# Quads of 512-column passes for the token-major blocks of a transformer layer kernel

## The chip, the core and the metric

One Trainium2 chip; the program runs on one of its cores. The metric is the device time of one execution in microseconds (us). A core has TensorE (PE in the rows; its weight loads are PEld), VectorE (DVE), ScalarE (ACT), GpSimd (POOL) and SyncE (SP), which here only issues DMAs. Matmuls write to PSUM, eight banks of 128 partitions by 512 fp32; ACT and DVE read those banks. The engines run their own instruction lists and wait for each other through semaphores.

## The reference

One layer on x of 512 tokens by 1024, all in fp32. One wide projection `h @ w_in` feeds three things: a sparse attention in four groups of four heads (compressed, selected and window keys), a state-space mixer in four groups of eight heads, and two gates. Then two projections are gated and merged, projected out, and a gated feed-forward with a short convolution follows.

```python
h = rms_norm(x, norm1_w[layer])
(q, k_c, v_c, k_s, v_s, k_w, v_w, g_nsa, z, xbc, dt_raw,
 gate_a, gate_b) = split_columns(h @ w_in[layer], IN_SIZES)
y_a = nsa_mixer(q, k_c, v_c, k_s, v_s, k_w, v_w, g_nsa, ...)
y_b = ssd_mixer(z, xbc, dt_raw, ...)
merged = sigmoid(gate_a) * (y_a @ w_proj_a[layer]) + sigmoid(gate_b) * (y_b @ w_proj_b[layer])
x = x + merged @ w_out[layer]
x = x + conv_glu_ffn(rms_norm(x, norm2_w[layer]), ...)
```

The parts of it that the change touches are the columns q, k_s, v_s, k_w, v_w (the "heads" columns of a group: 128 + 128 for q and 64 each for the rest, 512 in all) and z (512 columns a group), which are wanted with tokens on the partitions.

## The kernel before, in words

**Weights.** Every weight matrix is cut into units of 512 KB, numbered in the order of use. SP loads unit u into one of two tiles `wraw` (it waits until unit u-2 is split: `load`). ACT rounds it to fp32r (`hi(u)`, L1029, into one of four slots of `w_high`), DVE forms the rest (`lo(u)`, L1553, `w_low`), and TensorE multiplies three times for each product: high by high, high by low, low by high. `hi(u)` waits until the block that last used the slot is done, and the loaded unit.

**Blocks.** Most units are 128 output columns by 1024 rows and make one block: 8 k-steps of three matmuls of 512 tokens (`ktile`, L611 to L613), weights stationary, into one of the two banks `g`. Blocks whose result is wanted token-major come in pairs (`half_pair`, L652 to L654): activations stationary, and the moving operand is the 128 columns of two units side by side, 256 columns a matmul. A pair is done in two halves of 48 matmuls, each half giving two of the four token tiles for 256 columns. There are 16 such pairs: 5 and 8 before the groups, four in each of groups 0 to 2 (two for the heads columns of the next group, two for z) and two in group 3 (z only; its other four blocks of that place are gate columns, of the ordinary kind).

**A group.** The main stretch runs over g = 0..3, 14 blocks each: OB, OC, eight blocks OQ+n (n = 0..7, the *turns*), and four OX blocks. Between the k-steps of a block TensorE does the small work of the attention, at places set by dictionaries `between`. A turn n belongs to unit n of the attention (head r = n // 2 and kind br = n % 2), and runs as follows:

- TensorE: scores of unit n+1 (L786), k-step 0, values of unit n-1 (L802) before k-step 1, the first two pieces of the transposed probabilities before k-step 3 (seven transposes, L604; they wait for `p_ready`), the third piece before k-step 6 (three transposes). The pieces use two banks `t` in turn, so the third waits until DVE has read the first (`t_rel`). In turn 0 the places are 2 and 5, in turn 7 they are 5 and 7.
- ACT: rounds each piece (`pT_hi`, L1333), does the exponentials of unit n+1 (`exps`, L1296), one first tap of the convolution (L1103), copies the block's bank out (`evac_mid`), then `hi(u+3)`.
- DVE: `scale(n)` (reciprocal L1837, four products L1843; gives `p_ready`), `ttr(n+1)` (score maxima, L1784), in turns 2, 4, 6 `out_fold` (L1874), `lo(u0+4+n)`, `p_low` on the first two pieces (L1855), `p_low` on the third, and from turn 2 on one convolution (`conv`, three instructions, L1603), then the next turn.

The order on each engine is the order written; no scheduler moves anything. In groups 1 to 3 turn 0 follows the normalized output of the group before (`y_back_out`: four copies on ACT, each with a DMA that stores it).

## Time and profile before

| | us |
|---|---|
| median of 3 runs | 1240.8 (1240.5 to 1240.89) |
| the profiled execution | 1241.02 |
| its span, first to last instruction | 1239.3 |
| PE busy in the span | 1225.5 (99%) |
| DVE busy | 841.5 (68%) |
| ACT busy | 633.1 (51%) |

TensorE's granted clock is 1.0 of full speed through the span. A matmul's duration in the records includes its way through the array and overlaps the next one's, so the cost of a matmul in a dense run is the distance between two starts. The busy share of DVE is a mean over the program: in the 80 us of a group's turns from 400 to 480 us it is busy for 69.75 us.

### The profile page before, as it was taken

The page shows a single profiled execution, that of the slowest core. Times are in us where ns is not written, and L with a number is a line of the kernel's source. Part 1 is how long each engine was busy: PE and PEld are TensorE (multiplying, and loading weights), DVE is VectorE, ACT ScalarE, POOL GpSimd, SP SyncE. Part 2 cuts the span into 40 slices and gives each one's busy share as a digit, 9 for nine tenths or more (in the row PEclk, how much of TensorE's full clock was granted, in tenths as well). Part 3 has the DMA queues.
Part 4 walks back from the last instruction along what each step waited for, and adds up shares of the span by engine and source line. Part 5 has one row for each costly group of instructions (what it writes and reads, how often), then busy time and mean ns, then how long its engine had stood idle before and what let it go on. Part 6 is the DMA issues. An engine that isn't in the chain of part 4 may idle for free.

```text
span 1239.3 us, 17708 instructions
## 1 busy us (share of the span) xinstructions
PE 1225.5 (99%) x6725; PEld 1053.5 (85%) x6725; DVE 841.5 (68%) x1579; ACT 633.1 (51%) x1169; POOL 88.8 (7%) x78
## 2 busy tenths in 40 slices
PE   7999999999999999999999999999999999999998
PEld 6998998899978998889978888888888888888887
DVE  4526888898889887999774643333788888884221
ACT  6615777678785868676765633323432322332210
POOL 1000001400042001400040000000000000000000
PEclk9999999999999999999999999999999999999999
DMA  8612321142213221132216633335133333334341
GB/s 241 162 35 68 86 61 46 49 108 63 61 44 80 75 70 51 51 103 61 61 34 212 230 96 92 90 104 175 56 102 102 87 100 102 92 97 136 102 130 40
DMA packets 185737, 116.34 MB, mean 94 GB/s; under 512 B 25933, under 2 KB 169909, under 8 KB 185653
## 3 DMA queue, kind: packets, MB, share of 16 engines
q1 hardware_dynamic: 182023, 108.86, 30.5%
q10 hardware_dynamic: 3630, 6.35, 1.4%
q8 instruction: 54, 0.88, 0.3%
q14 instruction: 30, 0.25, 0.1%
HBM read 106.80 MB, written 8.39 MB: 93 GB/s over the span
## 4 chain that ended last, share of the span: by engine, by line
PE 94%; DVE 4%; ACT 1%; issue 0%; ACTq 0%; DVEq 0%
PE g L611 17%; PE g L613 16%; PE g L612 16%; PE t L604 5%; PE g L652 4%; PE g L654 4%; PE g L653 4%; PE ob L802 3%; PE s L786 3%; PE s L960 2%; PE s L961 2%; PE s L962 2%; PE s L883 1%; PE t L708 1%; PE ob L920 1%; PE t L962 1%
## 5 line engine op out<-in xcount | busy, mean ns | idle before, releaser
L1029 ACT ACTIVATE w_high<-wraw 128x1024 fp32r<-128x1024 f32 x175 | 185.1, 1058 | 281.4 <-DMA wraw<-in_ffn_w_up 135.2
L1553 DVE TENSOR_TENSOR w_low<-wraw,w_high 128x1024 fp32r<-128x1024 f32 x174 | 216.7, 1248 | 125.2 <-ACT w_high L1029 122.7
L611 PE MATMUL g<-hT_hi,w_high 128*128 128x512 f32 x360 | 158.3, 440 | 1.2 <-DVE hT_lo L1559 1.2
L652 PE MATMUL g<-w_high,hT_hi 128*128 128x256 f32 x512 | 151.6, 296 | 0.2 <-DVE w_low L1553 0.2
L654 PE MATMUL g<-w_high,hT_lo 128*128 128x256 f32 x512 | 144.7, 283 | 0.0
L653 PE MATMUL g<-w_low,hT_hi 128*128 128x256 f32 x512 | 144.6, 282 | 0.0
L613 PE MATMUL g<-hT_hi,w_low 128*128 128x512 f32 x360 | 141.2, 392 | 0.0
L612 PE MATMUL g<-hT_lo,w_high 128*128 128x512 f32 x360 | 140.8, 391 | 0.0
L611 PE MATMUL g<-h2T_hi,w_high 128*128 128x512 f32 x352 | 137.4, 390 | 0.1
L613 PE MATMUL g<-h2T_hi,w_low 128*128 128x512 f32 x352 | 137.0, 389 | 0.0
L612 PE MATMUL g<-h2T_lo,w_high 128*128 128x512 f32 x352 | 137.0, 389 | 0.0
L653 PEld LDWEIGHTS g<-w_low,hT_hi 128*128 128x128 f32 x512 | 97.8, 191 | 0.5
L652 PEld LDWEIGHTS g<-w_high,hT_hi 128*128 128x128 f32 x512 | 97.6, 191 | 0.7 <-issue 0.6
L654 PEld LDWEIGHTS g<-w_high,hT_lo 128*128 128x128 f32 x512 | 97.4, 190 | 0.0
L611 PEld LDWEIGHTS g<-hT_hi,w_high 128*128 128x128 f32 x360 | 67.9, 189 | 16.9 <-issue 7.1
L612 PEld LDWEIGHTS g<-hT_lo,w_high 128*128 128x128 f32 x360 | 68.0, 189 | 15.8 <-issue 5.7
L613 PEld LDWEIGHTS g<-hT_hi,w_low 128*128 128x128 f32 x360 | 67.6, 188 | 15.3
L1333 ACT ACTIVATE pT_hi<-t 128x384 fp32r<-128x384 f32 (+1 forms) x96 | 47.1, 525 | 62.6 <-PE t L604 62.6
L611 PEld LDWEIGHTS g<-h2T_hi,w_high 128*128 128x128 f32 x352 | 66.1, 188 | 14.8 <-issue 0.8
L613 PEld LDWEIGHTS g<-h2T_hi,w_low 128*128 128x128 f32 x352 | 66.1, 188 | 13.8
L612 PEld LDWEIGHTS g<-h2T_lo,w_high 128*128 128x128 f32 x352 | 66.1, 188 | 13.3
L1855 DVE TENSOR_TENSOR pT_lo<-t,pT_hi 128x384 fp32r<-128x384 f32 (+1 forms) x96 | 54.6, 596 | 30.0 <-ACT pT_hi L1333 29.9
(348 smaller groups left out, 2542.4 us busy)
## 6 DMA issues: line engine op xcount, KB each, us to landing
wraw<-in_w_in SPq DMA_DIRECT2D x152, 256.0 KB, 3.3
wraw<-in_ffn_w_up SPq DMA_DIRECT2D x88, 256.0 KB, 3.2
wraw<-in_ffn_w_down SPq DMA_DIRECT2D x44, 256.0 KB, 3.1
wraw<-in_w_proj_b SPq DMA_DIRECT2D x32, 256.0 KB, 3.1
yT_lo<-spill SPq DMA_DIRECT2D x6, 1024.0 KB, 10.5
spill<-piece_e ACTq DMA_DIRECT2D x16, 256.0 KB, 4.2
wraw<-in_w_proj_a SPq DMA_DIRECT2D x16, 256.0 KB, 3.1
wraw<-in_w_out SPq DMA_DIRECT2D x16, 256.0 KB, 3.4
```

What stands on the lines that cost most here:

```text
L604: last = nc.tensor.transpose(dst, src, ident[0:n, 0:n])
L611: nc.tensor.matmul(gb[par][:, :], w, hi, start=k == 0, stop=False)
L612: nc.tensor.matmul(gb[par][:, :], w, lo, start=False, stop=False)
L613: return nc.tensor.matmul(gb[par][:, :], wl, hi, start=False, stop=last)
L652: nc.tensor.matmul(out_, hT[0][:, k, cols], w, start=k == 0, stop=False)
L653: nc.tensor.matmul(out_, hT[0][:, k, cols], wl, start=False, stop=False)
L654: ins = nc.tensor.matmul(out_, hT[1][:, k, cols], w, start=False, stop=k == KD - 1)
L962: ins = nc.tensor.matmul(banks[i][:, :], lo, w[:, kk, :], start=False, stop=stop)
L1029: nc.scalar.activation(whi[slot_of(u)][:, :, :], wraw[u % 2][:, :, :], ACT.Copy).then_inc(w_hi, 1)
L1333: nc.scalar.activation(pT[0][:, offT[j]:offT[j] + w], tb[par][:, 0:w], ACT.Copy).then_inc(pT_hi, 1)
L1553: V.tensor_tensor(wlo[slot_of(u)][:, :, :], wraw[u % 2][:, :, :], whi[slot_of(u)][:, :, :].bitcast(F32), ALU.subtract).then_inc(w_lo, 1)
L1855: V.tensor_tensor(pT[1][:, offT[j]:offT[j] + w], tb[T_(K_UNIT[n] + j) % 2][:, 0:w], pT[0][:, offT[j]:offT[j] + w].bitcast(F32), ALU.subtra ...
```

## The change

The seven runs of four token-major blocks in the groups (heads columns in groups 0 to 2, z in all four) become quads. A quad has four units, each of 256 weight rows by all 512 columns; a matmul has a 128x128 tile of activations stationary and 512 columns moving. It still fills four turns (`quad_window`), 24 matmuls each: in the first two turns token tiles 0 and 1 in the two banks `g`, in the last two tiles 2 and 3. In the second turn of each pair the quarters of the two tiles are interleaved. The pairs 5 and 8 stay. With it:

- SP loads units by rows (`heads_rows`: three DMAs a unit, with pieces of 256 columns and of 64 columns; `z_rows`: two DMAs).
- ACT copies a bank out once per token tile, twice in each odd turn: the first tile behind the third piece of `pT_hi` (turns 1 and 5) or behind the second piece and its exponentials (turns 3 and 7), the second tile at the end. A heads tile takes three instructions (copy, two squares). The copy of block OC (`evac_x(g, 5)`) moves ahead of turn 0's first piece in groups 1 to 3.
- `hi` no longer follows each copy: two are done at the end of turns 2 and 6, one at the end of turns 0, 3, 4, 7, one in turn 0 and none in turns 1 and 5. A new semaphore `quad_rows` says when the first two units of a quad are free.
- DVE: `lo` of turns 1 and 5 stands before `ttr`, `lo` of turns 2 and 6 behind the convolution, the others where they were.

```diff
-PAIRS = {5, 8} | {U_GRP + GROUP_BLOCKS * g + o for g in range(G) for o in ((OQ, OQ + 2, OZ, OZ + 2) if g < G - 1 else (OZ, OZ + 2))}
+PAIRS = {5, 8}
+QUADS = [U_GRP + GROUP_BLOCKS * g + o for g in range(G) for o in (OQ, OZ) if g < G - 1 or o == OZ]
+def blocks_done(v):
+    for first in QUADS:
+        if first + 2 <= v < first + 4:
+            return first + 4
+    return v + (2 if v in PAIRS else 1)
+def quad_rows_over(v):
+    for k, first in enumerate(QUADS):
+        if first <= v < first + 2:
+            return 2 * k + v - first + 1
+    return 0
...
+            def heads_rows(u, g, q):
+                rows = slice(2 * P * q, 2 * P * (q + 1))
+                dst = wide(wraw[u % 2])
+                qw = io["w_in"][0, rows, C_Q + 256 * g:C_Q + 256 * (g + 1)]
+                kv = io["w_in"][0, rows, C_KS:C_KS + 4 * 256].rearrange("(k p) (s n) -> p k s n", p=P, s=4)
+                load(u, [(dst[:, :, 0:256], qw.rearrange("(k p) n -> p k n", p=P))] + [
+                    (dst[:, kk, 256:512].rearrange("p (s n) -> p s n", s=4), kv[:, kk, :, DH * g:DH * (g + 1)])
+                    for kk in range(2)])
...
-                        qkv(u0 + OQ + b, g + 1, b)
+                        heads_rows(u0 + OQ + b, g + 1, b)
...
+            def quad_window(u, n, between):
+                first, half = u - n, n % 2
+                a, b = (0, 1) if n < 2 else (2, 3)
+                c, d = 2 * half, 2 * half + 1
+                order = ((a, c), (b, c), (a, d), (b, d)) if n == 1 else ((a, c), (a, d), (b, c), (b, d))
+                for place, (i, q) in enumerate(order):
+                    if half == 0 and q == 0:
+                        pe.wait_ge(g_rel, first + i - 1)
+                    if i == 0:
+                        pe.wait_ge(w_lo, first + q + 1)
+                    w, wl = wide(whi[slot_of(first + q)]), wide(wlo[slot_of(first + q)])
+                    for kk in range(2):
+                        if 2 * place + kk in between:
+                            between[2 * place + kk]()
+                        h, l = (t[:, 2 * q + kk, P * i:P * (i + 1)] for t in hT)
+                        out_ = gb[(first + i) % 2][:, :]
+                        nc.tensor.matmul(out_, h, w[:, kk, :], start=q == 0 and kk == 0, stop=False)
+                        nc.tensor.matmul(out_, h, wl[:, kk, :], start=False, stop=False)
+                        ins = nc.tensor.matmul(out_, l, w[:, kk, :], start=False, stop=q == 3 and kk == 1)
...
+                    if n == 2 and i == 3:
+                        ins.then_inc(quad_rows, 1)
...
+                ROUND_END = {0: (3,), 2: (4, 5), 3: (6,), 4: (7,), 6: (8, 9), 7: (10,)}
...
+                    nc.scalar.activation(tokq[:, :, i, :], src, ACT.Copy)
+                    nc.scalar.activation(sq[:, :, i, :], src[:, 0:2, :], ACT.Square)
+                    nc.scalar.activation(sq_k[:, :, i, :], src[:, 2:4, 0:DH], ACT.Square).then_inc(g_rel, 1)
...
                 if g:
                     y_scale(g - 1)
                     y_back_out(g - 1)
+                    evac_x(g, 5, following=False)
...
+                        if n % 2 and j == (2 if n % 4 == 1 else 1):
+                            evac_tile(n, 0)
...
-                    evac_mid(n)
+                    if n < 4 and g == G - 1:
+                        evac_block(n)
+                    elif n % 2:
+                        evac_tile(n, 1)
+                    for q in ROUND_END.get(n, ()):
+                        hi(u0 + OQ + q)
...
                     scale(n)
+                    if n in (1, 5):
+                        lo(u0 + 4 + n)
                     if n < 7:
                         ttr(n + 1)
...
-                    lo(u0 + 4 + n)
+                    if n not in (1, 2, 5, 6):
+                        lo(u0 + 4 + n)
...
                     if n > 1:
                         conv(g, CONVS[n - 2])
+                    if n in (2, 6):
+                        lo(u0 + 4 + n)
```

Three places of the order. First DVE in turn 2 of a group, from the last score maximum (`negmx`) to the next turn's first instructions (`pscale`); before:

```order
L1784 ISA negmx 128x1
L1874 TENSOR_TENSOR hstage<-ob,hstage 64x512
L1553 TENSOR_TENSOR w_low<-wraw,w_high 128x1024
L1705 COPY kcg<-kcs 128x64
L1855 TENSOR_TENSOR pT_lo<-t,pT_hi 128x512
L1855 TENSOR_TENSOR pT_lo<-t,pT_hi 128x384 x2
L1603 SCALAR_TENSOR_TENSOR xcx<-xraw,pcol,xcx 128x511
L1603 SCALAR_TENSOR_TENSOR xcx<-xraw,pcol,xcx 128x510
L1603 SCALAR_TENSOR_TENSOR xcx<-xraw,pcol,xcx 128x509
L1837 RECIPROCAL pscale<-rsum 128x4
```

and now:

```order
L1872 ISA negmx 128x1
L1962 TENSOR_TENSOR hstage<-ob,hstage 64x512
L1793 COPY kcg<-kcs 128x64
L1943 TENSOR_TENSOR pT_lo<-t,pT_hi 128x512
L1943 TENSOR_TENSOR pT_lo<-t,pT_hi 128x384 x2
L1691 SCALAR_TENSOR_TENSOR xcx<-xraw,pcol,xcx 128x511
L1691 SCALAR_TENSOR_TENSOR xcx<-xraw,pcol,xcx 128x510
L1691 SCALAR_TENSOR_TENSOR xcx<-xraw,pcol,xcx 128x509
L1641 TENSOR_TENSOR w_low<-wraw,w_high 128x1024
L1925 RECIPROCAL pscale<-rsum 128x4
```

The split of a weight unit (`w_low`) has moved from before the pieces (`pT_lo`) to behind the convolution (`xcx`), directly before the next turn's `pscale`. Turn 6 is changed in the same way.

Second, ACT at the start of a group's turns, groups 1 to 3: `piece_e` is the copy of the last output tile, `bcraw` the copy of block OC, `pT_hi` the pieces of unit 0; before:

```order
L1170 DMA spill<-piece_e 128x512
L1333 ACTIVATE pT_hi<-t 128x512
L1333 ACTIVATE pT_hi<-t 128x384
L1095 ACTIVATE bcraw<-g 128x512
L1029 ACTIVATE w_high<-wraw 128x1024
L1333 ACTIVATE pT_hi<-t 128x384
```

and now:

```order
L1232 DMA spill<-piece_e 128x512
L1157 ACTIVATE bcraw<-g 128x512
L1411 ACTIVATE pT_hi<-t 128x512
L1411 ACTIVATE pT_hi<-t 128x384
L1091 ACTIVATE w_high<-wraw 128x1024
L1411 ACTIVATE pT_hi<-t 128x384
```

The copy of the bank now stands before the first piece. Third, ACT in turn 3 of groups 0 to 2 (`chan`, `sq` and `junk` are the copies and squares of the heads columns); before:

```order
L1333 ACTIVATE pT_hi<-t 128x512
L1333 ACTIVATE pT_hi<-t 128x384
L1296 ACTIVATE piece_b,rsum<-piece_a,negmx 128x512
L1296 ACTIVATE piece_b,rsum<-piece_a,negmx 128x384
L1333 ACTIVATE pT_hi<-t 128x384
L1296 ACTIVATE piece_b,rsum<-piece_a,negmx 128x256
L1296 ACTIVATE piece_b,rsum<-piece_a,negmx 128x128
L1103 ACTIVATE xcx<-xraw,pcol 128x512
L1111 ACTIVATE chan<-g 128x2x256
L1113 ACTIVATE junk<-g 128x2x128
L1029 ACTIVATE w_high<-wraw 128x1024
```

and now:

```order
L1411 ACTIVATE pT_hi<-t 128x512
L1411 ACTIVATE pT_hi<-t 128x384
L1373 ACTIVATE piece_b,rsum<-piece_a,negmx 128x512
L1373 ACTIVATE piece_b,rsum<-piece_a,negmx 128x384
L1287 ACTIVATE chan<-g 128x4x128
L1288 ACTIVATE sq<-g 128x2x128
L1289 ACTIVATE junk<-g 128x2x64
L1411 ACTIVATE pT_hi<-t 128x384
L1373 ACTIVATE piece_b,rsum<-piece_a,negmx 128x256
L1373 ACTIVATE piece_b,rsum<-piece_a,negmx 128x128
L1165 ACTIVATE xcx<-xraw,pcol 128x512
L1287 ACTIVATE chan<-g 128x4x128
```

A token tile is copied out ahead of the third piece, and another at the end of the turn.

## Rows read from the trace of the kernel before

**Rows 1.** The page, busy time and share of the span: TensorE.

```profile
PE 1225.5 (99%) x6725; PEld 1053.5 (85%) x6725; DVE 841.5 (68%) x1579; ACT 633.1 (51%) x1169; POOL 88.8 (7%) x78
```

**Rows 2.** Timeline (start us, us, what): scores at starts of turns, groups 2 and 3.

```profile
416.70 0.40 PE L786 MATMUL s<-khh,qs 128*128 128x512 f32 x1
426.32 0.40 PE L786 MATMUL s<-khh,qs 128*128 128x512 f32 x1
...
552.55 0.40 PE L786 MATMUL s<-khh,qs 128*128 128x512 f32 x1
561.99 0.39 PE L786 MATMUL s<-khh,qs 128*128 128x512 f32 x1
```

**Rows 3.** Timeline of PE, group 2: third pieces, turns 1 to 6; first piece, 7.

```profile
414.05 0.49 PE L604 MATMUL t<-ident,piece_b 128*128 128x128 f32 x3
...
424.56 0.49 PE L604 MATMUL t<-ident,piece_b 128*128 128x128 f32 x3
...
433.93 0.49 PE L604 MATMUL t<-ident,piece_b 128*128 128x128 f32 x3
...
443.86 0.52 PE L604 MATMUL t<-ident,piece_b 128*128 128x128 f32 x3 [0.16 <-DVE pT_lo L1855]
...
453.44 0.52 PE L604 MATMUL t<-ident,piece_b 128*128 128x128 f32 x3
...
463.08 0.49 PE L604 MATMUL t<-ident,piece_b 128*128 128x128 f32 x3
...
469.71 0.93 PE L604 MATMUL t<-ident,piece_b 128*128 128x128 f32 x7
```

**Rows 4.** Timeline of DVE, group 2, turns 2 to 4.

```profile
425.61 0.56 DVE L1855 TENSOR_TENSOR pT_lo<-t,pT_hi 128x384 fp32r<-128x384 f32 x1 [0.89 <-ACT pT_hi L1333]
...
428.31 0.17 DVE L1837 RECIPROCAL pscale<-rsum 128x4 f32<-128x4 f32 x1
...
429.90 0.68 DVE L1784 CUSTOM_DVE_ANT_0 piece_a<-s,hbias 128x512 f32<-128x512 f32 x1
...
431.55 1.22 DVE L1553 TENSOR_TENSOR w_low<-wraw,w_high 128x1024 fp32r<-128x1024 f32 x1
432.69 1.15 DVE L1855 TENSOR_TENSOR pT_lo<-t,pT_hi 128x512 fp32r<-128x512 f32 x2
...
443.02 1.16 DVE L1855 TENSOR_TENSOR pT_lo<-t,pT_hi 128x512 fp32r<-128x512 f32 x2
```

**Rows 5.** Timeline of ACT, group 2, around turn 0's first piece, and turn 3's.

```profile
401.43 0.33 ACTq L1170 DMA_DIRECT2D spill<-piece_e  x1
401.81 0.98 ACT L1333 ACTIVATE pT_hi<-t 128x512 fp32r<-128x512 f32 x2 [0.48 <-PE t L604]
402.67 0.61 ACT L1095 ACTIVATE bcraw<-g 128x512 f32<-128x512 f32 x1
...
434.46 0.49 ACT L1333 ACTIVATE pT_hi<-t 128x384 fp32r<-128x384 f32 x1 [0.54 <-PE t L604]
```

**Rows 6.** Timeline of DVE, turn 0 and 1 of group 2, and turn 1 of group 3.

```profile
402.51 1.16 DVE L1855 TENSOR_TENSOR pT_lo<-t,pT_hi 128x512 fp32r<-128x512 f32 x2
...
412.84 1.15 DVE L1855 TENSOR_TENSOR pT_lo<-t,pT_hi 128x512 fp32r<-128x512 f32 x2
...
548.99 1.15 DVE L1855 TENSOR_TENSOR pT_lo<-t,pT_hi 128x512 fp32r<-128x512 f32 x2
```

**Rows 7.** Timeline of PE and ACT, group 3, turns 1 to 3.

```profile
549.92 0.49 PE L604 MATMUL t<-ident,piece_b 128*128 128x128 f32 x3
...
560.26 0.49 PE L604 MATMUL t<-ident,piece_b 128*128 128x128 f32 x3
...
562.76 0.58 ACT L1215 ACTIVATE chan<-g 128x512 f32<-128x512 f32 x1
563.24 1.06 ACT L1029 ACTIVATE w_high<-wraw 128x1024 fp32r<-128x1024 f32 x1
...
569.46 0.49 PE L604 MATMUL t<-ident,piece_b 128*128 128x128 f32 x3
```

More of the change, by code:

```diff
@@ L72, with last_in_slot, loads_to @@
 X0_UNITS = (7, 10, 11, 12)
-PAIRS = {5, 8} | {U_GRP + GROUP_BLOCKS * g + o for g in range(G) for o in ((OQ, OQ + 2, OZ, OZ + 2) if g < G - 1 else (OZ, OZ + 2))}
+PAIRS = {5, 8}
+QUADS = [U_GRP + GROUP_BLOCKS * g + o for g in range(G) for o in (OQ, OZ) if g < G - 1 or o == OZ]
 def slot_of(u):
     return (u if u < PRE_BLOCKS else u + 1) % SLOTS
-def done_for_slot(u):
+def last_in_slot(u):
     before = [v for v in range(u) if slot_of(v) == slot_of(u)]
-    if not before:
-        return 0
-    return before[-1] + (2 if before[-1] in PAIRS else 1)
+    return before[-1] if before else None
+def loads_to(u):
+    heads = [first + q for first in QUADS if (first - U_GRP) % GROUP_BLOCKS == OQ for q in range(4)]
+    return sum(48 if v in heads else 32 for v in range(u % 2, u + 1, 2))
+def blocks_done(v):
[8 more added lines that the diff above has]
+    return 0
 class Count:
@@ L264, in program @@
         w_hi, w_lo, mm_done, g_rel = sem("w_hi"), sem("w_lo"), sem("mm_done"), sem("g_rel")
+        quad_rows = sem("quad_rows")
         x_loaded = [sem(f"x_loaded{i}") for i in range(NT)]
@@ L426, in qkv, with wide_load, z_rows @@
                 sides(u, w_in_cols(g * DH + k, DH), DH, w_in_cols(g * DH + v, DH), DH)
+            def wide_load(u, w, kq, h):
+                v = w[2 * P * kq:2 * P * (kq + 1), D // 2 * h:D // 2 * (h + 1)].rearrange("(k p) n -> p k n", p=P)
+                load(u, [(wide(wraw[u % 2])[:, kk, :], v[:, kk, :]) for kk in range(2)])
+            def heads_rows(u, g, q):
[6 more added lines that the diff above has]
+                    for kk in range(2)])
+            def z_rows(u, g, q):
+                wide_load(u, io["w_in"][0, :, C_Z + 512 * g:C_Z + 512 * (g + 1)], q, 0)
             def x_in(u, g, q):
@@ L452, in _ @@
                 for b in range(4):
-                    halves(u0 + OZ + b, w_in_cols(g * 512 + (C_Z + P * b)))
+                    z_rows(u0 + OZ + b, g, b)
                 for q in range(4):
@@ L482, in _ @@
                     halves(m * 3 + (U_MRG + q), w[:, m * P:(m + 1) * P])
-            def wide_load(u, w, kq, h):
-                v = w[2 * P * kq:2 * P * (kq + 1), D // 2 * h:D // 2 * (h + 1)].rearrange("(k p) n -> p k n", p=P)
-                load(u, [(wide(wraw[u % 2])[:, kk, :], v[:, kk, :]) for kk in range(2)])
             def out_unit(q):
@@ L860, in _ @@
                     u = u0 + OQ + n
-                    if u in PAIRS or u - 1 in PAIRS:
-                        half_pair(u, n % 2, between)
+                    if n >= 4 or g < G - 1:
+                        quad_window(u, n % 4, between)
                     else:
@@ L1024, in hi @@
             def hi(u):
-                if done_for_slot(u):
-                    act.wait_ge(mm_done, done_for_slot(u))
-                act.wait_ge(w_loaded[u % 2], 32 * (u // 2 + 1))
+                v = last_in_slot(u)
+                if v is not None:
+                    if quad_rows_over(v):
+                        act.wait_ge(quad_rows, quad_rows_over(v))
+                    else:
+                        act.wait_ge(mm_done, blocks_done(v))
+                act.wait_ge(w_loaded[u % 2], loads_to(u))
                 nc.scalar.activation(whi[slot_of(u)][:, :, :], wraw[u % 2][:, :, :], ACT.Copy).then_inc(w_hi, 1)
@@ L1336, in _ @@
                         if n == 0 and j == 1:
-                            evac_x(g, 5)
+                            if g:
+                                hi(u0 + OQ + 2)
+                            else:
+                                evac_x(g, 5)
+                        if n % 2 and j == (2 if n % 4 == 1 else 1):
+                            evac_tile(n, 0)
                         if n == 0 and j == 2:
@@ L1905, in _ @@
                     if n == 7 and g < G - 1:
-                        dve.wait_ge(g_rel, u0 + OQ + 2)
+                        dve.wait_ge(g_rel, u0 + OQ + 4)
                         q_sums()
```

32 lines of the change are left out of this document (20 added, 12 removed).

## The prediction, made before the changed kernel had run

> **What bounds the kernel now.** I read the page first: TensorE is busy for 99% of the span [rows 1], so it looks like the bound everywhere, and a cheaper matmul should be worth its whole price. That is a mean over a long program, and since a matmul's record overlaps the next one's, gaps under 0.1 us or so do not show in it. So I then laid the timelines of PE, DVE and ACT beside each other for one group's eight turns and asked, at the three places of a turn where TensorE waits (first pieces for `p_ready`, third piece for `t_rel`, first product for the weights), how much earlier the awaited work was done.
>
> The marks I use are the starts of the third pieces [rows 3]. From turn to turn they stand 10.51, 9.37, 9.93, 9.58 and 9.64 us apart. The third piece of turn 4 carries a wait for DVE (0.16 us shown). Its `p_low` started at 443.02 [rows 4] and the piece 0.84 us later [rows 3]. Putting the same 0.84 behind the others' `p_low`: turn 1, 412.84 + 0.84 = 413.68 against 414.05 [rows 3, 6], 0.37 us spare; turn 3, 432.69 + 0.84 = 433.53 against 433.93 [rows 3, 4], 0.40 spare. So in the turns TensorE and DVE are bound nearly together: DVE holds turn 4 (and, by the length of its three transposes, 0.52 as in turn 4 and not 0.49, turn 5), and is 0.4 us behind elsewhere. A saving on TensorE counts only up to that, and a move on DVE counts from there on.
>
> **Part 1, the passes.** 28 turns (7 quads of 4) change from 48 matmuls of 256 columns to 24 of 512; the columns are the same. Before shows both kinds in the same turn: from the scores of turn 1 to those of turn 2 group 2 (256) takes 426.32 - 416.70 = 9.62 us, group 3 (gates, 512) 561.99 - 552.55 = 9.44 [rows 2]. The saving is 0.18 us a turn, 0.0225 a k-step, if nothing else binds; over 28 turns 5.0 us. That row has weights stationary and the quads have activations stationary, so I bound it by 0 and by twice as much (10 us), and take 0.18, the same place in the same program.
>
> The Trainium skill, "TensorE: Matmul & The Clock Gate", section "Back-to-back issue gap", gives a warm gap of N/2.4 + 2.5 ns: 109.2 ns for 256 columns and 215.7 for 512, so a pair of the former against one of the latter saves 2.6 ns. By it an estimate of the saving is 672 x 2.6 ns = 1.7 us instead of 5.0. The rows' 0.18 us in 24 matmuls is 7.5 ns each, three times the rule, and the sum goes by the rows.
>
> **Part 2, DVE's split behind the convolution (turns 2 and 6).** Before, DVE stood idle 0.89 us for the third piece of turn 2 [rows 4] after it had done the split; now the split comes after that idle time and stands in the chain from one third piece to the next. The chain from 424.56 [rows 3]: to the next `scale` 428.31 - 424.56 = 3.75 (rounding on ACT, `p_low`, convolution); the split 432.69 - 431.55 = 1.14; `scale` 429.90 - 428.31 = 1.59; `ttr` and turn 3's own split to `p_low` 432.69 - 429.90 = 2.79; 0.84 to the piece [rows 4]. Sum 10.11 us, where TensorE took 9.37. So the third piece of turn 3 comes 0.74 us later after that of turn 2 than before, and TensorE waits there. Behind it are queued that turn's last k-steps and the whole next turn. From turn 3 to 4, 9.93 us, is DVE's already and is unchanged (same instructions). From turn 4 to 5, 9.58, the split only changes places with `ttr`: unchanged.
>
> At turn 6 the same move meets more room: next to bind are turn 7's first pieces, which wait for `scale(7)`: 3.75 + 1.14 + 1.59 + 0.14 (hand-over: 0.84 less the 0.70 of the first `p_low`, taken alone) = 6.62 us after the third piece of turn 6, against 469.71 - 463.08 = 6.63 before [rows 3]. So -0.01, while TensorE by itself could have saved 0.16.
>
> **Part 3, ACT's order.** In groups 1 to 3 the copy of block OC comes ahead of the first piece. ACT showed 0.48 us idle there, but inside it lies the issue of a DMA from 401.43 for 0.33 us [rows 5], so the piece started 0.05 us after ACT was free. The copy takes 0.47 to 0.61 (the latter its record). `pT_hi` then ends near 402.9 in place of 402.4, and `p_low`, at 402.51 [rows 6], starts some 0.40 later. DVE has no pause from there to turn 1, so its third piece can come at 413.68 + 0.40 = 414.08, not at the 413.73 that 14 cheaper k-steps (0.32) would allow. Bounds: 0 and 0.6.
>
> In turn 3 a tile's copy, three instructions (estimate 0.95 us from a copy of 0.47, a square of 256 and one of 128 columns), stands before the third piece, where 0.54 us was idle [rows 5]. By itself that would be 0.4 us late. But the third piece now waits for DVE for about 0.6 us longer after the first ones, and that hides it: cost nothing, and 0.4 us a group if Part 2 is wrong. In turn 1 the tile's copy stands before the compressed copies, whose next reader, the values of turn 2, has about 1 us left. The banks: tile 2 opens at turn 2 behind 1.2 us of scores, tile 0 was copied in turn 1. No wait.
>
> In group 3 turn 2 the split needs the rounded unit, and the copy of the gate block stays before it: the rounding ended at 563.24 + 1.06 = 564.30, which is 4.04 us after the third piece [rows 7], and now the split wants it at 3.75. With 0.05 for the semaphore the chain there is 10.11 + 0.34 = 10.45, against 569.46 - 560.26 = 9.20 [rows 7]. In groups 0 to 2 that copy is gone from turn 2 and the rounding is in time.
>
> **Part 4, loads.** Same bytes, 26 more DMAs or so. A split later in turns 2 and 6 also lets SP's load of the unit two further start later; that unit is wanted half a turn or more after it lands. Nothing.
>
> **The sum, at the third pieces.** Groups 0, 1 and 2, taken from group 2: turn 1 +0.03 (414.08 - 414.05); to turn 2 -0.18; to turn 3 +0.74; to 4 and 5 nothing; to 6 -0.18; to turn 7's first -0.01; the last three k-steps -0.07. That is +0.33 us each, +1.0. Group 3 (its first four turns had 512 columns before): turn 1, DVE 548.99 + 0.84 + 0.40 = 550.23 against 549.92 [rows 6, 7], +0.31; to turn 3 +1.25; to 5 and 6 -0.18 each (no heads sums there, so turn 5 is TensorE's); -0.01 and -0.07: +1.1. In all +2.1 us. The profiled execution took 1241.02 us, so 1243.1; it lies 0.2 above the median of 1240.8, which makes 1242.9.
>
> **Rivals.**
> A, the forecast: DVE takes the saving and a little more. 1242.9, in itself 1240.5 to 1245.5: the split's move may cost 0 to 1.14 in each of eight places, of which I count 0.74 in three and 0.91 in one.
> B, the passes pay: DVE and ACT keep ahead and all 5.0 us arrive: 1235.8. For it: TensorE's 99%, and the wait shown in each group is only 0.16 us at turn 4 and a little more in turn 1. Against it: the chain of 10.11 us, of measured pieces. It decides if DVE's chain from turn 2 to 3 is under 9.2 us.
> C, ACT becomes the bound (slower): in turns 1 and 3 of groups 0 to 2 the tile's copy of 0.95 us before the exponentials (turn 1) or the third piece (turn 3) pushes `scale` and `p_low` by its full length: 6 x 0.95 = 5.7 more, 1248.6. Against it: 0.4 us spare by idle, and TensorE waiting for DVE anyway. It decides once ACT's third piece starts over 0.6 us after its transposes.
> D, the change doesn't do what it says: 512 columns over stationary activations cost as much as two of 256. The savings of 0.44 us a group in the sum go, +1.7: 1244.6.
> E, loads late: the heads units now all hold 256-byte pieces (64 columns), where two of four did. If two of them in each of three groups land 1 us late on TensorE's path, 6 us more, 1248.9. The Trainium skill, "DMA: Bandwidth & Descriptors", section "Specifications", asks for 512 B or more for line rate, which speaks for E; no row in my list bears on it, and the sum does not use it.
>
> **How the numbers follow.** 0.2% is 2.5 us, about what can be told from no change here: faster is under 1238.3, slower over 1243.3. Chances: A 0.66 (0.42 within, 0.22 above, 0.02 below), B 0.11, C 0.14, D 0.05 (0.03 above), E 0.04. Faster 0.13, same 0.44, slower 0.43. The range leaves about a tenth out on each side: below it half of B and more, above it most of C and E: 1237.5 to 1247.5.
>
> **What would show it.** In the profile after: 24 matmuls of 512 at turn 1 with the turn 0.18 us shorter (Part 1); third pieces of turns 2 and 3 10.1 us apart in groups 0 to 2 and 10.4 in group 3, with DVE's `p_low` as releaser, and DVE idle before turn 2's third piece for about 2 us (Part 2); 9.9 from turn 3 to 4; turn 7's first pieces 6.6 after turn 6's third; the first `pT_hi` of turn 0 0.4 us later after its DMA (Part 3). Third pieces 9.2 us apart at turn 3 would make me wrong towards B; waits of TensorE for ACT's copies (`g_rel`) or for `w_low` at a turn's start would mean C or E.

## The result, and the profile after

| | before | after |
|---|---|---|
| median of 11 runs, us | 1240.89 (1240.5 to 1241.36) | 1243.94 (1243.64 to 1244.18) |
| the profiled execution | 1241.02 | 1243.97 |
| its span | 1239.3 | 1242.2 |

The ratio is 1.0024, 95% interval 1.0016 to 1.0031: slower by 3.05 us, a quarter of a percent, where +2.1 was forecast (1242.9, range 1237.5 to 1247.5). One timing of the run a_bc_back below, 5590.46 us, was a slow one and is left aside; its other ten lie between 1242.47 and 1243.28. The page's first line looks like that of [rows 1] but for fewer matmuls and 2.4 us less of busy TensorE, in a span 2.9 us longer:

```profile
PE 1223.1 (98%) x6053; PEld 1013.7 (82%) x6053; DVE 842.5 (68%) x1579; ACT 633.7 (51%) x1181; POOL 88.4 (7%) x78
```

TensorE got cheaper and waits more. Here is the wait of TensorE that has grown in the changed kernel (columns: waiting line, what it waited for, us in total, times, longest):

```profile
PE t L637 <- DVE pT_lo L1943: 5.7, 19, 0.4
```

The same first wait in the kernel before, the one that a third piece of transposes has for DVE's low part:

```profile
PE t L604 <- DVE pT_lo L1855: 1.7, 8, 0.3
```

From 1.7 to 5.7 us, at 19 places instead of 8 (in both kernels four of them are transposes of `cs` behind turn 1's third piece). No line of the list of TensorE's waits names a bank copy of a tile or a weight load. The places are in the timeline of TensorE, group 2, third pieces of turns 0 to 6 (they answer [rows 3]):

```profile
404.64 0.52 PE L637 MATMUL t<-ident,piece_b 128*128 128x128 f32 x3
...
414.96 0.52 PE L637 MATMUL t<-ident,piece_b 128*128 128x128 f32 x3 [0.27 <-DVE pT_lo L1943]
...
425.35 0.49 PE L637 MATMUL t<-ident,piece_b 128*128 128x128 f32 x3
...
435.44 0.52 PE L637 MATMUL t<-ident,piece_b 128*128 128x128 f32 x3 [0.40 <-DVE pT_lo L1943]
...
445.40 0.52 PE L637 MATMUL t<-ident,piece_b 128*128 128x128 f32 x3 [0.34 <-DVE pT_lo L1943]
...
454.98 0.52 PE L637 MATMUL t<-ident,piece_b 128*128 128x128 f32 x3 [0.21 <-DVE pT_lo L1943]
...
464.45 0.49 PE L637 MATMUL t<-ident,piece_b 128*128 128x128 f32 x3
```

Turns 2 and 3 now stand 435.44 - 425.35 = 10.09 us apart, not 9.37. DVE's timeline of that stretch shows why (it answers [rows 4]; the step to the next turn is the `RECIPROCAL`):

```profile
423.76 1.16 DVE L1943 TENSOR_TENSOR pT_lo<-t,pT_hi 128x512 fp32r<-128x512 f32 x2
426.40 0.56 DVE L1943 TENSOR_TENSOR pT_lo<-t,pT_hi 128x384 fp32r<-128x384 f32 x1 [1.49 <-ACT pT_hi L1411]
426.88 2.31 DVE L1691 SCALAR_TENSOR_TENSOR xcx<-xraw,pcol,xcx 128x511 f32<-128x511 f32 x3
429.10 1.22 DVE L1641 TENSOR_TENSOR w_low<-wraw,w_high 128x1024 fp32r<-128x1024 f32 x1
430.24 0.17 DVE L1925 RECIPROCAL pscale<-rsum 128x4 f32<-128x4 f32 x1
...
434.62 1.15 DVE L1943 TENSOR_TENSOR pT_lo<-t,pT_hi 128x512 fp32r<-128x512 f32 x2
```

DVE stands idle for 1.49 us before the third low part (0.89 before), and then does the split, 1.14 us to the next start, on the way to the next turn. Before, the split was done ahead of these pieces. About 2 us of idle time were forecast here, the old 0.89 and the split's 1.14; only 0.60 were added, because the two low parts ahead of it now start 425.35 - 423.76 = 1.59 us before TensorE's third piece instead of 0.98.

In group 3 the first pieces of turn 3 already wait, 0.44 us for DVE's products, and the third piece again (0.40).

Distances over a group's turns, us, all from starts of pieces on TensorE ("first" is turn 0's first piece, the last two marks are turn 7's), and the change in each group:

| stretch | group 2 before | after | change g0 | g1 | g2 | g3 | forecast g0 to g2 | g3 |
|---|---|---|---|---|---|---|---|---|
| first to third of turn 1 | 13.05 | 13.18 | -0.06 | +0.23 | +0.13 | +0.76 | +0.03 | +0.31 |
| 1 to 2 | 10.51 | 10.39 | -0.15 | -0.16 | -0.12 | +0.03 | -0.18 | 0 |
| 2 to 3 | 9.37 | 10.09 | +0.72 | +0.70 | +0.72 | +1.21 | +0.74 | +1.25 |
| 3 to 4 | 9.93 | 9.96 | +0.02 | +0.04 | +0.03 | +0.02 | 0 | 0 |
| 4 to 5 | 9.58 | 9.58 | 0 | -0.01 | 0 | -0.17 | 0 | -0.18 |
| 5 to 6 | 9.64 | 9.47 | -0.20 | -0.18 | -0.17 | -0.18 | -0.18 | -0.18 |
| 6 to first of 7 | 6.63 | 6.62 | 0 | 0 | -0.01 | 0 | -0.01 | -0.01 |
| to last of 7 | 2.20 | 2.22 | +0.01 | +0.02 | +0.02 | +0.02 | -0.07 | -0.07 |

The columns add up to +0.34, +0.64, +0.60 and +1.69, in all +3.27 us (the forecast's columns to +2.11). What lies outside them gives back 0.37 and leaves the 2.9 of the spans. Of the 0.37, 0.17 lie before the first mark (128.47 before, 128.30 after). They are not the change's work: b_late_split, whose program is that of the kernel before up to there, has the mark at 128.30 too.

Turn 1's row comes from the low part of turn 0's first piece. Turn 0 of group 2, on ACT, then on DVE (they answer [rows 5, 6]):

```profile
402.17 0.33 ACTq L1232 DMA_DIRECT2D spill<-piece_e  x1
402.61 0.60 ACT L1157 ACTIVATE bcraw<-g 128x512 f32<-128x512 f32 x1 [0.55 <-ACT piece_e L1253]
403.10 0.98 ACT L1411 ACTIVATE pT_hi<-t 128x512 fp32r<-128x512 f32 x2
```

```profile
403.80 1.15 DVE L1943 TENSOR_TENSOR pT_lo<-t,pT_hi 128x512 fp32r<-128x512 f32 x2 [0.37 <-ACT pT_hi L1411]
```

The rounding of the first piece starts 403.10 - 402.61 = 0.49 behind the copy, and the low part 403.80 - 401.78 = 2.02 us after TensorE's first piece (its start is 401.78), where it had been 402.51 - 401.00 = 1.51. In group 3 the same low part:

```profile
540.84 1.16 DVE L1943 TENSOR_TENSOR pT_lo<-t,pT_hi 128x512 fp32r<-128x512 f32 x2 [0.74 <-ACT pT_hi L1411]
```

TensorE's first piece started at 538.45 there, so 2.39 us, where it had been 538.67 - 537.12 = 1.55. Of these 0.84 us, 0.5 are the bank copy again. The rest is that ACT's last output copy before it started 0.03 us ahead of the first piece, and 0.41 ahead in group 2; I did not follow where that comes from, and a_bc_back, with the copy moved back, still has this row at +0.28 in group 3.

### The profile page after: what moved, and what is told of

It is laid out like the page before. It is cut to its first block, busy times and chain, and to the rows that moved or that the text cites. A ratio compares the mean times of both kernels' runs of the same rounds, so it can differ in the third digit from the quotient of the medians.

```text
span 1242.2 us, 16367 instructions
## 1 busy us (share of the span) xinstructions
PE 1223.1 (98%) x6053; PEld 1013.7 (82%) x6053; DVE 842.5 (68%) x1579; ACT 633.7 (51%) x1181; POOL 88.4 (7%) x78
## 4 chain that ended last, share of the span: by engine, by line
PE 83%; DVE 13%; ACT 3%; issue 1%; ACTq 0%; DVEq 0%
PE g L644 16%; PE g L646 16%; PE g L645 16%; PE t L637 4%; DVE w_low L1641 3%; DVE piece_a L1872 2%; PE g L707 2%; PE g L709 2%; PE g L708 2%; DVE pT_lo L1943 2%; DVE xcx L1691 2%; PE ob L860 2%; PE s L1020 2%; PE s L1019 2%; PE s L1018 2%; PE s L844 2%
## 5 line engine op out<-in xcount | busy, mean ns | idle before, releaser
L707 PE MATMUL g<-w_high,hT_hi 128*128 128x512 f32 x224 | 95.3, 425 | 0.0
L709 PE MATMUL g<-w_high,hT_lo 128*128 128x512 f32 x224 | 88.2, 394 | 0.0
L708 PE MATMUL g<-w_low,hT_hi 128*128 128x512 f32 x224 | 87.8, 392 | 0.0
L644 PE MATMUL g<-yT_hi,w_high 128*128 128x512 f32 x192 | 74.7, 389 | 0.0
L645 PE MATMUL g<-yT_lo,w_high 128*128 128x512 f32 x192 | 74.7, 389 | 0.0
L646 PE MATMUL g<-yT_hi,w_low 128*128 128x512 f32 x192 | 74.7, 389 | 0.0
```

Of the source, the lines that this page charges most:

```text
L644: nc.tensor.matmul(gb[par][:, :], w, hi, start=k == 0, stop=False)
L645: nc.tensor.matmul(gb[par][:, :], w, lo, start=False, stop=False)
L646: return nc.tensor.matmul(gb[par][:, :], wl, hi, start=False, stop=last)
L707: nc.tensor.matmul(out_, h, w[:, kk, :], start=q == 0 and kk == 0, stop=False)
L708: nc.tensor.matmul(out_, h, wl[:, kk, :], start=False, stop=False)
L709: ins = nc.tensor.matmul(out_, l, w[:, kk, :], start=False, stop=q == 3 and kk == 1)
```

## The experiments

Each was timed in five rounds beside the kernel before, whose median in the three sets was 1240.90, 1240.67 and 1240.88.

| run | median us | ratio to before, 95% |
|---|---|---|
| b_late_split | 1244.48 | 1.0029 (1.0018 to 1.0041) |
| a_early_split | 1255.48 | 1.0119 (1.0105 to 1.0133) |
| a_bc_back | 1243.1 | 1.0017 (1.0007 to 1.0026) |
| a_early_bc | 1254.39 | 1.011 (1.0096 to 1.0124) |
| a_mid_split | 1239.73 | 0.9991 (0.9982 to 1.0) |
| a_mid_bc | 1238.64 | 0.9983 (0.9975 to 0.9992) |
| b_short_conv | 1238.61 | 0.9982 (0.9973 to 0.9991) |
| a_short_conv | 1238.96 | 0.9986 (0.9977 to 0.9995) |
| a_between | 1235.53 | 0.9956 (0.9943 to 0.9968) |
| b_between | 1239.42 | 0.9987 (0.9978 to 0.9996) |
| a_short_halves | 1242.47 | 1.0013 (1.0004 to 1.0022) |
| a_rows_plain | 1243.69 | 1.0022 (1.0013 to 1.0031) |

**b_late_split: only DVE's move, in the kernel before.**

```diff
-                    lo(u0 + 4 + n)
+                    if n not in (2, 6):
+                        lo(u0 + 4 + n)
...
                         conv(g, CONVS[n - 2])
+                    if n in (2, 6):
+                        lo(u0 + 4 + n)
```

> The kernel before with one edit: DVE's split of the weight unit in turns 2 and 6 stands behind the convolution. No pass, load or ACT instruction changes. Theory A (DVE's chain is what the change lengthened): the third pieces of turns 2 and 3 stand 10.1 us apart in groups 0 to 2 (9.37 before) and 10.4 in group 3 (9.20), turn 6 costs nothing, so 3 x 0.73 + 1.2 = +3.4 us: 1244.3. Rival 'DVE had idle time, so the move is free': 1240.9 and 9.4 us between those pieces.

Measured 1244.48. Group 2, TensorE, third pieces of turns 2 to 4:

```profile
426.04 0.49 PE L604 MATMUL t<-ident,piece_b 128*128 128x128 f32 x3
...
436.14 0.52 PE L604 MATMUL t<-ident,piece_b 128*128 128x128 f32 x3 [0.34 <-DVE pT_lo L1855]
...
446.10 0.52 PE L604 MATMUL t<-ident,piece_b 128*128 128x128 f32 x3 [0.15 <-DVE pT_lo L1855]
```

10.10 us between the first two, and in group 3 572.67 - 562.57 = 10.10 (10.4 was expected). Moving one instruction in each of eight turns, without a quad in the kernel, costs 3.6 us, more than the whole change. The run also shows a small cost at turn 6's end that I had at nothing: TensorE's first pieces of turn 7 take longer, and turn 7's first to its third piece stand 474.20 - 471.95 = 2.25 us apart, where it was 2.20.

```profile
471.95 0.98 PE L604 MATMUL t<-ident,piece_b 128*128 128x128 f32 x7
...
474.20 0.49 PE L604 MATMUL t<-ident,piece_b 128*128 128x128 f32 x3
```

**a_bc_back: ACT's copy of block OC back behind the second piece in groups 1 to 3.**

```diff
                     y_back_out(g - 1)
-                    evac_x(g, 5, following=False)
...
                         if n == 0 and j == 1:
-                            if g:
-                                hi(u0 + OQ + 2)
-                            else:
-                                evac_x(g, 5)
+                            evac_x(g, 5)
```

> The changed kernel with ACT's copy of block OC back behind the second piece of turn 0 in groups 1 to 3. Theory: the first low part of turn 0 comes 0.5 us sooner after its pieces, and the third piece of turn 1 stands 9.9 us behind that of turn 0 instead of 10.32, 3 x 0.4 = 1.2 us less: 1242.7. Rival: TensorE's quad wants that bank at k-step 4 of turn 0 and waits for the copy there, and the gain is lost: 1243.9 or more, with a wait for the copy at turn 0.

Measured 1243.1: 0.84 us less than the changed kernel, of the 1.2 expected. The third piece of turn 1 now stands 9.87 us behind turn 0's in all of groups 1 to 3 (group 2: 414.81 - 404.94). But turn 0 gives some back. TensorE in turn 0 of group 2, the first matmul of k-steps 3 and 4:

```profile
403.30 0.40 PE L707 MATMUL g<-w_high,hT_hi 128*128 128x512 f32 x1
...
404.13 0.50 PE L707 MATMUL g<-w_high,hT_hi 128*128 128x512 f32 x1
```

K-step 4 starts 0.83 us behind k-step 3; in the changed kernel it was 403.93 - 403.24 = 0.69. It opens the other bank, and the copy that frees it runs on ACT from 403.47. These 0.14 us are what the rival said would come; that they are a wait for the copy is inferred from the times, since no releaser is shown beside the matmul.

**a_early_split, and with the copy back, a_early_bc.**

```diff
-                order = (...) if n == 1 else (...)
+                order = (...) if n in (1, 2) else (...)
...
-                ROUND_END = {0: (3,), 2: (4, 5), 3: (6,), 4: (7,), 6: (8, 9), 7: (10,)}
+                ROUND_END = {0: (3,), 2: (5,), 3: (6,), 4: (7,), 6: (9,), 7: (10,)}
...
-                        if 0 < n < 7 and j == 1:
+                        if n in (2, 6) and j == 1:
+                            hi(u0 + OQ + n + 2)
+                            exps(n + 1, (3,))
+                        elif 0 < n < 7 and j == 1:
                             exps(n + 1, (3, 2))
...
-                        exps(n + 1, (1, 0))
+                        exps(n + 1, (2, 1, 0) if n in (2, 6) else (1, 0))
...
-                    if n not in (1, 2, 5, 6):
+                    if n not in (1, 5):
                         lo(u0 + 4 + n)
...
-                    if n in (2, 6):
-                        lo(u0 + 4 + n)
```

> The changed kernel with the split of turns 2 and 6 back before the third piece's low part, in DVE's idle time there. For that the unit must be rounded half a turn sooner: TensorE takes k-steps of turns 2 and 6 in the order that turn 1 has (both tiles over the first weight unit, then both over the second), which frees that unit's slot at k-step 3, and ACT rounds behind the second piece, with one exponential moved behind the third. Theory A: third pieces of turns 2 and 3 about 9.2 us apart in all groups, turn 4's third piece 18.9 us after turn 2's (20.05 in the changed kernel), so 3 x 1.15 + 1.4 = 4.9 us less than 1243.9: 1239.0. Rival 'ACT is late': the rounding, 1.06 us, pushes the third piece's copy and the next exponentials, and third pieces of turns 2 and 3 stay 9.8 apart: 1242. Rival 'the loss lies in the loads or the bank copies': stays at 1243.9.

> The two edits of the changed kernel together (early split in turns 2 and 6, and the copy of OC behind the second piece). They act in different turns, so by theory A their gains add: 1243.9 - 4.9 - 1.2 = 1237.8. If TensorE becomes the bound in turn 1 or if one edit takes the other's idle time, 1239.

Measured 1255.48 and 1254.39. All my theories missed, and the fault was mine: the split was put ahead of all three low parts, and DVE works its list in order. DVE in turn 2 of group 2:

```profile
431.42 1.22 DVE L1644 TENSOR_TENSOR w_low<-wraw,w_high 128x1024 fp32r<-128x1024 f32 x1 [1.54 <-ACT w_high L1091]
```

It sits 1.54 us at the split, which waits for a rounding that ACT only does behind the first two pieces, with low parts queued behind it that had been ready. TensorE pays at the third piece:

```profile
433.49 0.52 PE L637 MATMUL t<-ident,piece_b 128*128 128x128 f32 x3 [1.82 <-DVE pT_lo L1946]
```

A wait put ahead of ready work in two turns of each group makes the kernel 11.5 us slower than the change. The copy's edit still was worth 1.1 us on top.

**a_mid_split: the split between the low parts of the second and third piece.** The k-step order of turns 2 and 6 and the earlier rounding on ACT are those of a_early_split; DVE's list differs from the changed kernel by this and by the split that is gone behind the convolution.

```diff
-                    p_low(n, range(3) if n else (2,))
+                    if n in (2, 6):
+                        p_low(n, (0, 1))
+                        lo(u0 + 4 + n)
+                        p_low(n, (2,))
+                    else:
+                        p_low(n, range(3) if n else (2,))
```

> As a_early_split, but DVE's split of turns 2 and 6 stands between the low parts of the second and the third piece and not ahead of all three, so that the first two do not wait for the rounding. In a_early_split they did (up to 1.85 us at the third piece, 19.2 us in all). Theory A: the third piece's wait is gone, turns 2 and 3 about 9.3 us apart at their third pieces, turn 4's 18.9 to 19.2 after turn 2's; 3 to 5 us less than 1243.9: 1239.8. Rival 'ACT is late': third pieces 9.8 apart, 1242.

Measured 1239.73. DVE in turn 2 of group 2: the split lies in what was idle time.

```profile
422.06 1.16 DVE L1946 TENSOR_TENSOR pT_lo<-t,pT_hi 128x512 fp32r<-128x512 f32 x2
423.55 1.22 DVE L1644 TENSOR_TENSOR w_low<-wraw,w_high 128x1024 fp32r<-128x1024 f32 x1 [0.34 <-ACT w_high L1091]
424.69 0.55 DVE L1946 TENSOR_TENSOR pT_lo<-t,pT_hi 128x384 fp32r<-128x384 f32 x1
```

And TensorE's third pieces of turns 2 to 4:

```profile
423.61 0.49 PE L637 MATMUL t<-ident,piece_b 128*128 128x128 f32 x3
...
432.81 0.49 PE L637 MATMUL t<-ident,piece_b 128*128 128x128 f32 x3
...
443.08 0.52 PE L637 MATMUL t<-ident,piece_b 128*128 128x128 f32 x3 [0.68 <-DVE pT_lo L1946]
```

9.20 us from turn 2 to 3 (as expected, and 0.17 under the kernel before), but 19.47 from 2 to 4, where 18.9 to 19.2 was expected. The part from 3 to 4 has grown from 9.93 to 10.27 or 10.28 us in groups 0 to 2, and not in group 3 (9.93), where turn 3 has no token tile to copy out. ACT and DVE in turn 3 of group 2, then DVE in turn 3 of group 3:

```profile
432.76 0.59 ACT L1287 ACTIVATE chan<-g 128x512 f32<-128x512 f32 x1
...
433.65 0.51 ACT L1411 ACTIVATE pT_hi<-t 128x384 fp32r<-128x384 f32 x1
...
434.20 0.56 DVE L1946 TENSOR_TENSOR pT_lo<-t,pT_hi 128x384 fp32r<-128x384 f32 x1 [1.29 <-ACT pT_hi L1411]
```

```profile
569.93 0.56 DVE L1946 TENSOR_TENSOR pT_lo<-t,pT_hi 128x384 fp32r<-128x384 f32 x1 [0.97 <-ACT pT_hi L1411]
```

With the tile's copy ahead of it, ACT rounds the third piece 433.65 - 432.81 = 0.84 us behind TensorE's start. DVE's low part stands 434.20 - 432.81 = 1.39 us behind it, and in group 3 569.93 - 568.88 = 1.05. These 0.34 us in each of three groups are the price that the forecast had named for the copy in turn 3 (0.4 us a group if Part 2 is wrong): hidden behind DVE in the changed kernel, it shows once DVE's chain is shorter.

**a_mid_bc: both edits.**

> a_mid_split with the copy of block OC behind the second piece of turn 0 in groups 1 to 3, which alone gave 0.8 us. If they add: 1239.0. If the time won at turn 1 only meets the same DVE chain later, 1239.8, as a_mid_split.

Measured 1238.64: they add (1.1 us more). It is faster than both kernels.

**a_between and b_between: the split between the pieces in turns 3 and 4 too, with and without quads.** In both the split stands between the low parts in the turns `n in (2, 3, 4, 6)`. a_between stands on a_mid_bc (which had it there in turns 2 and 6), b_between on the kernel before with nothing else touched.

> a_mid_bc with DVE's split between the low parts of the second and third piece in turns 3 and 4 too (turns 2, 3, 4 and 6). In a_mid_bc DVE is idle for 1.30 us there in turn 3 and 0.76 in turn 4, while TensorE waits 0.7 us for it at turn 4's third piece. Theory (DVE's place, not its load, costs): that wait goes and the passes' saving shows in turns 2 to 7, 3 us less than a_mid_bc: 1235.6. Rival 'DVE's load binds': the work is the same, so 1238.6.

> The kernel before with the same place for DVE's split in turns 2, 3, 4 and 6 (its rounding is early enough there as it is). No wide passes, so TensorE's own pace holds it: only the stall at turn 4 and its surroundings go, 1239.2. The difference to a_between, 3.6 us expected, is what the quads are worth once DVE is out of the way. If the quads are worth nothing even then, both come out alike.

Measured 1235.53 and 1239.42. TensorE's third pieces of turns 2 to 5 in a_between, group 2:

```profile
421.16 0.49 PE L637 MATMUL t<-ident,piece_b 128*128 128x128 f32 x3
...
430.33 0.49 PE L637 MATMUL t<-ident,piece_b 128*128 128x128 f32 x3
...
439.73 0.49 PE L637 MATMUL t<-ident,piece_b 128*128 128x128 f32 x3
...
449.29 0.52 PE L637 MATMUL t<-ident,piece_b 128*128 128x128 f32 x3 [0.20 <-DVE pT_lo L1942]
```

9.17, 9.40 and 9.56. Its wait line has shrunk to

```profile
PE t L637 <- DVE pT_lo L1942: 1.9, 8, 0.3
```

The difference of the two kernels, 3.9 us, is what the quads are worth, with the copies, loads and roundings that come with them, when DVE is out of the way. They do pay, and in the change as made DVE's list, for the most part, took it all. a_between is 5.4 us faster than the kernel before and 8.4 faster than the change.

**b_short_conv and a_short_conv: DVE's convolution cut to 64 columns** (the other columns of it are left out).

```diff
-V.scalar_tensor_tensor(y_[:, s:T], x_[:, 0:T - s], w[3 - s], y_[:, s:T], ALU.mult, ALU.add)
+V.scalar_tensor_tensor(y_[:, s:s + 64], x_[:, 0:64], w[3 - s], y_[:, s:s + 64], ALU.mult, ALU.add)
```

> The kernel before with the convolution's three steps on 64 columns in place of 509 to 511 (left out of the computation: the rest of those columns). This takes about 1.2 us or more from DVE in each of turns 2 to 7 and nothing from TensorE, so it shows TensorE's own pace in the turns. Theory: only DVE's small stalls go (0.16 us at turn 4 and what is near it), 1239.5 to 1240.5. If DVE did not bind anywhere, 1240.9.

> The changed kernel with the same shortened convolution. Theory A: the chain from turn 2 to 3 falls below TensorE's time, and the passes' saving of 0.15 to 0.18 us a turn shows in turns 2 to 7 of all groups: 2 to 3 us faster than b_short_conv (turn 1 keeps its loss of 0.2 to 0.5 in groups 1 to 3), 1237.5. Rival D (512 columns cost what two of 256 cost): no faster than b_short_conv, 1240. Rival C (ACT's bank copies bind): still 1243.

Measured 1238.61 and 1238.96. The first lies 0.9 under what was expected, because DVE had held more than turn 4: there 9.93 us became 9.61, and the stretch behind it, 9.58 before, became 9.38. The expected 2 to 3 us between the two kernels did not come, and by the medians alone rival D would look right; the stretches tell otherwise. TensorE, group 2, third pieces of turns 2 to 5, first b_short_conv, then a_short_conv:

```profile
423.34 0.49 PE L604 MATMUL t<-ident,piece_b 128*128 128x128 f32 x3
...
432.72 0.49 PE L604 MATMUL t<-ident,piece_b 128*128 128x128 f32 x3
...
442.33 0.49 PE L604 MATMUL t<-ident,piece_b 128*128 128x128 f32 x3
...
451.71 0.49 PE L604 MATMUL t<-ident,piece_b 128*128 128x128 f32 x3
```

```profile
422.50 0.49 PE L637 MATMUL t<-ident,piece_b 128*128 128x128 f32 x3
...
432.42 0.52 PE L637 MATMUL t<-ident,piece_b 128*128 128x128 f32 x3 [0.40 <-DVE pT_lo L1943]
...
441.88 0.49 PE L637 MATMUL t<-ident,piece_b 128*128 128x128 f32 x3
...
451.06 0.49 PE L637 MATMUL t<-ident,piece_b 128*128 128x128 f32 x3
```

From 3 to 4 and 4 to 5 the quads take 9.46 and 9.18 against 9.61 and 9.38: the saving of 0.15 to 0.20 a turn is there. From 2 to 3 it is 9.92 against 9.38, although the convolution is short. DVE and ACT of a_short_conv in that turn say what holds it:

```profile
424.02 0.92 DVE L1691 SCALAR_TENSOR_TENSOR xcx<-xraw,pcol,xcx 128x64 f32<-128x64 f32 x3
426.07 1.23 DVE L1641 TENSOR_TENSOR w_low<-wraw,w_high 128x1024 fp32r<-128x1024 f32 x1 [1.13 <-ACT w_high L1091]
```

```profile
424.99 2.00 ACT L1091 ACTIVATE w_high<-wraw 128x1024 fp32r<-128x1024 f32 x2
```

DVE waits 1.13 us for the rounding. Beside b_short_conv, the stretch from turn 2 to 3 costs 2.9 us over the four groups (0.54 to 0.56 each in groups 0 to 2, 1.23 in group 3), and turn 1 another 1.0 (0.77 of it in group 3). They take what the passes give, and the two medians come out 0.35 apart. In the changed kernel two chains run from the third piece to the split, one over the convolution and one over ACT's exponentials, first tap and rounding, and they end within 0.2 us of each other (the split starts 3.75 us behind the third piece there, 3.57 here). Shortening one uncovers the other: the stretch only falls from 10.09 to 9.92 us, and in group 3 not at all (10.41). My chain was right as a length; that the convolution was what made it was half of the truth. The 5.0 us by which a_short_conv is faster than the changed kernel come almost all from other stretches (in group 2, 9.96 to 9.46 from turn 3 to 4 and 9.58 to 9.18 behind it).

**a_short_halves: the price of the width alone.**

```diff
+                        whole, two = (slice(0, 512),), (slice(0, 256), slice(256, 512))
+                        first_, last_ = q == 0 and kk == 0, q == 3 and kk == 1
+                        for c in whole if first_ else two:
+                            nc.tensor.matmul(out_[:, c], h, w[:, kk, c], start=first_, stop=False)
+                        for c in two:
+                            nc.tensor.matmul(out_[:, c], h, wl[:, kk, c], start=False, stop=False)
+                        for c in whole if last_ else two:
+                            ins = nc.tensor.matmul(out_[:, c], l, w[:, kk, c], start=False, stop=last_)
```

> a_short_conv with 22 of the 24 passes of each bank of a quad cut in two of 256 columns (same columns, order, loads and copies; the first and the last pass of a bank stay whole). It prices the width alone. Theory (7.5 ns for each pass): 22 x 8 / 4 = 44 more a turn pair, 0.165 us a turn in the 5 of 7 turns that TensorE bounds, 3.3 us over four groups: 1242.3. By the Trainium skill, page 'TensorE: Matmul & The Clock Gate', section 'Back-to-back issue gap', 2.6 ns each: 1240.1. If width does not matter: 1239.0.

Measured 1242.47, 3.5 us more than a_short_conv. Group 2, third pieces of turns 4 and 5:

```profile
444.17 0.49 PE L637 MATMUL t<-ident,piece_b 128*128 128x128 f32 x3
...
453.54 0.49 PE L637 MATMUL t<-ident,piece_b 128*128 128x128 f32 x3
```

9.37 us against 9.18. Of the 24 passes in this stretch 23 are cut (the last pass of one bank lies in it): 0.19 / 23 = 8.3 ns each where TensorE binds, each cut also adding a weight load. Over the program 3.5 us for 28 x 22 = 616 cut passes is 5.7 ns, since DVE hides a part. Rival D is out, and so is the price of 2.6 ns (1240.1 was expected by it).

**a_rows_plain: the heads' loads in longer pieces** (the key and value columns are other columns of the same matrix).

```diff
-                kv = ... C_KS:C_KS + 4 * 256].rearrange("(k p) (s n) -> p k s n", p=P, s=4)
+                kv = ... C_KS:C_KS + 256].rearrange("(k p) n -> p k n", p=P)
...
-                    (dst[:, kk, 256:512].rearrange("p (s n) -> p s n", s=4), kv[:, kk, :, DH * g:DH * (g + 1)])
+                    (dst[:, kk, 256:512], kv[:, kk, :])
```

> The changed kernel with the heads' key and value columns loaded from 256 columns side by side in pieces of 1 KB in place of four of 256 bytes (so other columns of the weights than the layer wants; their contents are the part that differs), the same number of transfers. Theory: no load is late, 1243.9 within 0.3. Rival E (short pieces delay a load on TensorE's path): 1 to 6 us less.

Measured 1243.69, 0.25 us below the change's median, with ranges that overlap (1243.37 to 1244.11 against 1243.64 to 1244.18). Rival E is out.

## Why the prediction was right, point by point

**What bounds the turns.** Right. TensorE's 98% hides that DVE's list sets the pace at turns 1, 3, 4 and 5: 19 waits for `pT_lo`, and moving DVE's instructions cost 3.6 us by itself (b_late_split). Moving them otherwise, with the k-step order and ACT's instructions changed to allow it, gave 4.2 us against the changed kernel (a_mid_split); two more turns of the same and OC's copy moved back made it 8.4 (a_between).

**Part 1, 0.18 us a turn.** Right in size: 5 to 6 in four groups gives 0.17 to 0.20, and a cut pass costs 8.3 ns against the 7.5 taken. At turn 2 it came with 0.12 to 0.16 in groups 0 to 2. In group 2 the loss is in the first of the eight k-steps, which lies ahead of a wait for DVE that both kernels have:

```profile
415.71 0.44 PE L604 MATMUL t<-ident,cs 128*128 128x128 f32 x2 [0.24 <-DVE pT_lo L1855]
```

```profile
416.66 0.44 PE L637 MATMUL t<-ident,cs 128*128 128x128 f32 x2 [0.26 <-DVE pT_lo L1943]
```

From there to turn 2's third piece it was 424.56 - 415.71 = 8.85 us and is 425.35 - 416.66 = 8.69: 0.16, as seven k-steps of 0.0225 make it. In turn 7's last stretch -0.07 was counted, for three k-steps of which two lie ahead of the mark, and +0.02 came; there the saving is not missing but taken back by Part 2's move. b_late_split, without a quad, makes the stretch 0.05 longer (2.25); a_mid_split, with quads and without the move, makes it 0.05 shorter (2.15). To have the split of turn 6 cost this stretch nothing was a term put at zero without a row for it. Together the two rows are 0.49 us of the 1.16 by which the marks came out above the forecast.

The Trainium skill ("TensorE: Matmul & The Clock Gate", section "Back-to-back issue gap") would have 2.6 ns a pass by its formula, which it gives for an isolated matmul; the measurement decides against it here. Both widths are slower here than the formula says: in turn 0 of the kernel before 14 distances of 256-column starts go from 402.16 to 403.83, 0.119 us each, and in the changed kernel a k-step of three passes of 512 takes 0.69 us, 0.230 each.

**Part 2, the chain of 10.11 us.** Right: 10.08 to 10.10 in groups 0 to 2, 10.41 in group 3 (10.45 forecast), 9.96 behind it, and 6.62 at turn 7. b_late_split shows the move alone as the cause of the 10.1. In group 3 it gives 10.10 too, without quads, so the other 0.31 there are the rounding, which ends too late for the split, as the forecast had it; a_short_conv, with the convolution cut, leaves that stretch at 10.41. In the sum of the forecast it is the largest term, 3 x 0.74 + 1.25 = 3.5 us; measured 3 x 0.71 + 1.21 = 3.35.

**Part 3, ACT's order.** The mechanism was right and the size too small. The low part came 0.51 us later in group 2 and not 0.40, which makes +0.13 in place of +0.03. In group 1 it came 0.54 later, and TensorE's third piece had less to spare than in group 2, from which the forecast had taken it: +0.23. In group 3 it came 0.84 later, which makes +0.76 in place of +0.31; the spare there, 0.09 us, had been read rightly. Group 0, where the copy was not moved, should not have been taken like the others: it lost nothing (-0.06). These four entries (-0.09, +0.20, +0.10, +0.45 beside the forecast) are 0.66 us of the miss, the largest part of it, and the step that was mis-sized. The tiles' copies cost nothing visible in the changed kernel: no releaser in the wait list is one of them, and in turn 3 of group 2 ACT rounds the third piece 436.00 - 435.44 = 0.56 us behind its start, under the 0.6 at which rival C would begin. So C is out for this kernel, for the reason given, TensorE waiting for DVE anyway. It is not out for the better ones: in a_mid_split the copy in turn 3 costs 0.34 us a group.

**Part 4.** Right (a_rows_plain).

**The sum.** +2.1 was forecast at the marks, +3.27 came there (+0.34, +0.64, +0.60, +1.69 against 0.33, 0.33, 0.33 and 1.1), less 0.37 outside the turns, of which 0.17 had come before the first one and 0.12 behind the last; I had counted nothing there. The 0.17 are no effect of the change (they stand in the one trace of the kernel before), so it was luck that they made the miss at the marks look smaller in the span.

**Rival B** failed for the reason given, the 10.1 us chain, and the decisive point was well placed: with the chain at 9.2 (a_mid_split) the kernel is 0.9 us faster than before, at the edge of what the runs can tell, and with turn 4's wait gone too (a_between) it is at 1235.5. That is near B's 1235.8, but not by B's sum: b_between shows 1.5 us of it without any quad, and the quads bring 3.9, not 5.0.
